# A recurrent layer's values centred as they are turned, and its output normalised without centring products

## The reference, cut to what matters

```python
state = (state * w_t[:, :, None, :] - sa[..., None] * b_t[:, :, None, :]
         + v_t[..., None] * k_t[:, :, None, :])
y_t = jnp.einsum('bhij,bhj->bhi', state, r_t)
...
mean = jnp.mean(y, axis=-1, keepdims=True)
var = jnp.mean(jnp.square(y - mean), axis=-1, keepdims=True)
y = ((y - mean) * lax.rsqrt(var + GN_EPS) * ln_w + ln_b)
bonus = jnp.sum(rh * kh * r_k, axis=-1, keepdims=True) * vh
y = (y + bonus)
return (y * jax.nn.silu(gate)) @ w_out
```

## Time and profile before

| | us |
|---|---|
| median of three runs | 1164.13 (1163.91 to 1165.45) |
| the profiled execution, its own time | 1166.54 |
| its span in the trace | 1164.4 |
| PE busy / DVE / ACT / POOL | 1130.5 / 733.9 / 608.5 / 466.5 |
| value and gate slots, then the scan's first corner | 160 to 253.8 |
| scan | 253.8 to 329.0 |
| norm stage, to the end of RWO slot 0 | 329.0 to 361.7 |

### The profile page before, as it was taken

The page is one execution under the profiler, slowest core; times in us unless marked ns, Lnnn a source line. Parts: engine busy times, 40 slices in busy tenths (PEclk is TensorE's granted clock), DMA queues, the critical chain, the costliest instruction groups (busy, mean ns, idle before and its releaser), DMA issues.

```text
span 1164.4 us, 19410 instructions
## 1 busy us (share of the span) xinstructions
PE 1130.5 (97%) x7558; PEld 888.3 (76%) x7558; DVE 733.9 (63%) x1166; ACT 608.5 (52%) x1026; POOL 466.5 (40%) x375
## 2 busy tenths in 40 slices
PE   7999999989999999999999999999999999999998
PEld 5756768878867887777777778878888888867776
DVE  6769997966675456666666484473593334567763
ACT  6867445535754466565655554462211344566563
POOL 2341024556733444333332344444454455532240
PEclk9999999999999999999999999999999999999999
DMA  8912447343183632212222123533333333322111
GB/s 279 278 55 73 88 112 219 107 136 82 45 282 99 193 105 78 85 56 73 60 68 73 55 91 92 165 90 88 98 102 91 103 97 91 91 73 67 61 55 73
DMA packets 194684, 123.02 MB, mean 106 GB/s; under 512 B 27877, under 2 KB 181030, under 8 KB 194214
## 3 DMA queue, kind: packets, MB, share of 16 engines
q1 hardware_dynamic: 191990, 119.27, 34.9%
q10 hardware_dynamic: 2608, 2.56, 0.7%
HBM read 105.03 MB, written 16.78 MB: 105 GB/s over the span
## 4 chain that ended last, share of the span: by engine, by line
PE 39%; issue 24%; POOL 12%; DVE 9%; ACT 1%; DMA 1%; POOLq 0%; ACTq 0%; SPq 0%; DVEq 0%
POOL b_w_lo L672 12%; PE banks L760 9%; PE banks L762 9%; PE banks L761 9%; DVE b_problems L2389 2%; DVE b_sum_squares L2387 2%; PE banks L1422 1%; PE banks L1020 1%; PE banks L767 1%; DVE b_a_lo L2218 1%; PE banks L1440 1%; DVE b_h_t L2214 1%; DMA b_problems<-d_a 1%; PE banks L1412 1%; PE banks L1039 1%
## 5 line engine op out<-in xcount | busy, mean ns | idle before, releaser
L672 POOL TENSOR_TENSOR b_w_lo<-b_w_raw,b_w_hi 128x512 fp32r<-128x512 f32 x296 | 401.0, 1376 | 635.6 <-ACT b_w_hi L1519 635.5
L760 PE MATMUL banks<-b_a_lo,b_w_hi 128*128 128x512 f32 x1232 | 492.5, 400 | 8.1 <-POOL b_w_lo L672 3.7
L762 PE MATMUL banks<-b_a_hi,b_w_lo 128*128 128x512 f32 x1232 | 481.6, 391 | 0.0
L761 PE MATMUL banks<-b_a_hi,b_w_hi 128*128 128x512 f32 x1232 | 480.5, 390 | 0.0
L1519 ACT ACTIVATE b_w_hi<-b_w_raw 128x1024 fp32r<-128x1024 f32 x156 | 165.1, 1058 | 259.6 <-PE banks L762 253.2
L760 PEld LDWEIGHTS banks<-b_a_lo,b_w_hi 128*128 128x128 f32 x1232 | 231.9, 188 | 70.0 <-issue 14.0
L762 PEld LDWEIGHTS banks<-b_a_hi,b_w_lo 128*128 128x128 f32 x1232 | 231.5, 188 | 50.2
L761 PEld LDWEIGHTS banks<-b_a_hi,b_w_hi 128*128 128x128 f32 x1232 | 232.1, 188 | 45.6 <-issue 0.5
L1957 ACT ACTIVATE b_exps<-banks,b_stats 128x128 f32<-128x128 f32 (+3 forms) x64 | 33.3, 525 | 67.4 <-DVE b_stats L2656 67.4
L2512 DVE SCALAR_TENSOR_TENSOR b_a_lo<-b_x_t,b_params,b_a_hi 128x512 fp32r<-128x512 f32 x32 | 34.3, 1086 | 23.5 <-ACT b_a_hi L1859 23.5
L2654 DVE TENSOR_TENSOR banks<-banks,b_consts 128x256 f32<-128x256 f32 x32 | 13.8, 433 | 45.8 <-PE banks L1269 44.7
(11 more groups left out here) (358 smaller groups left out, 1568.2 us busy)
## 6 DMA issues: line engine op xcount, KB each, us to landing
b_w_raw<-rw_w_in SPq DMA_DIRECT2D x32, 512.0 KB, 4.4
b_w_raw<-da_w_in SPq DMA_DIRECT2D x32, 512.0 KB, 4.1
b_w_raw<-w_in_a SPq DMA_DIRECT2D x32, 512.0 KB, 4.0
b_w_raw<-pe_w_gate SPq DMA_DIRECT2D x16, 512.0 KB, 4.2
d_ple<-b_ple_out SPq DMA_DIRECT2D x16, 256.0 KB, 4.2
b_w_raw<-rw_w_out SPq DMA_DIRECT2D x8, 512.0 KB, 4.2
b_ple_in<-d_ple SPq DMA_DIRECT2D x2, 2048.0 KB, 10.2
b_w_raw<-da_w_out SPq DMA_DIRECT2D x8, 512.0 KB, 3.9
```

What stands on the lines that cost most here:

```text
L672: m = pool.tensor_tensor(WLO[:, u % 2, ks], WRAW[:, u, ks], WHI[:, u % 2, ks].bitcast(F32), ALU.subtract)
L760: pe.matmul(dst, hi, a_lo[:, k_act, :], start=first, stop=False)
L761: pe.matmul(dst, hi, a_hi[:, k_act, :], start=False, stop=False)
L762: return pe.matmul(dst, lo, a_hi[:, k_act, :], start=False, stop=last)
```

## The change

The values are centred where they are turned: `turn_v` now multiplies the tile of values by the table `center` (the identity less 1/64 within each head) in place of a transposition by the identity, so what comes out is turned and free of its mean over each head. The bonus still takes the uncentred `TMP`. The eight products with `center` behind the scan are gone with their banks; ACT squares `YT` itself, and DVE multiplies `YT` by gain and gate in place. PE's embeddings are put in another order: 2 and 3 among the two sums of squares, 4 and 5 ahead of the wait for the root, 6 and 7 as before. ACT keeps embedding 2 ahead of the root. DVE does two gated bonuses ahead of the root instead of four, and the others one by one behind it.

```diff
@@ PE, turn_v
-            turn_four(BANK[6 - 2 * (j % 2)], [TMP[:, j % 2, t * P:(t + 1) * P] for t in range(TT)]).then_inc(sem("v_turn_mm"), 1)
+            for t in range(TT):
+                m = pe.matmul(BANK[6 - 2 * (j % 2)][:, t * P:(t + 1) * P], TMP[:, j % 2, t * P:(t + 1) * P], cst("center"),
+                              start=(t == 0), stop=(t == TT - 1), skip_group_check=True)
+            m.then_inc(sem("v_turn_mm"), 1)
@@ PE, behind the scan
-        for j in range(NT):
-            if j == NT - 1:
-                pe.wait_ge(sem("gn_kept"), 1)
-            if j in (2, 5):
-
-                pe.wait_ge(sem("bank_free"), RUN_RWO[1] - (1 if j == 2 else 0))
-            pe.matmul(gn_bank(j), center, YT[:, j, :], start=True, stop=True).then_inc(sem("gn_center"), 1)
-        for b in range(2):
-            gn_sums(b)
-        pe.wait_ge(sem("gn_kept"), NT)
-        for n in range(2, 5):
-            second_embedding(n)
+        second_embedding(2)
+        gn_sums(0)
+        second_embedding(3)
+        gn_sums(1)
+        pe.wait_ge(sem("bank_free"), RUN_RWO[1])
+        second_embedding(4)
+        second_embedding(5)
...
-        second_embedding(5)
         second_embedding(6)
@@ ACT
+        act.wait_ge(sem("y_even"), 2 * NC)
+        act.wait_ge(sem("y_odd"), 2 * NC)
         for j in range(NT):
-            act.wait_ge(sem("gn_center"), j + 1)
-            act.activation(GSQ[:, j, :], gn_bank(j), ACT.Square).then_inc(sem("gn_squared"), 1)
+            act.activation(GSQ[:, j, :], YT[:, j, :], ACT.Square).then_inc(sem("gn_squared"), 1)
+        keep_second(2)
         act.wait_ge(sem("gn_mm"), 2)
@@ DVE
-            stt(out=YT[:, j, :], in0=gn_bank(j), scalar=prm(LN_W, j), in1=GT[:, j, :], op0=ALU.mult, op1=ALU.mult
+            stt(out=YT[:, j, :], in0=YT[:, j, :], scalar=prm(LN_W, j), in1=GT[:, j, :], op0=ALU.mult, op1=ALU.mult
...
-        for j in range(4):
+        for j in range(2):
             gated_bonus(j)
...
-        gated_bonus(4)
+        gated_bonus(2)
...
-            if k + 5 < NT:
-                gated_bonus(k + 5)
+            if k + 3 < NT:
+                gated_bonus(k + 3)
```

More of the change, by code:

```diff
@@ L184, in sb_bank @@
     return (0, 1, 7)[i] if i < 3 else (i - 3) % 2
-def gn_tile_bank(j):
-    return (0, 1, 2, 3, 4, 5, 7, 0)[j]
 def block_rows(h, b):
@@ L357, in blocks_of @@
         return TRI0[rows_, c, :, cols] if c < 2 else TRI1[rows_, c - 2, :, cols]
-    def gn_bank(j):
-        return BANK[gn_tile_bank(j)]
     def chunk(c):
@@ L1156, in _ @@
         pe.wait_ge(sem("y_odd"), 2 * NC)
-        center = cst("center")
         def gn_sums(b):
@@ L1844, in _, with keep_second @@
         keep_y(NC - 1)
+        def keep_second(n):
+            act.wait_ge(sem("mm_done"), RUN_PLE[1][1] + n + 1)
+            if n >= 4:
+                act.wait_ge(sem(f"ple_out{n % 4}"), 48)
+            act.activation(P1OUT[:, n % 4, :], BANK[SECOND_BANKS[n]], ACT.Copy).then_inc(sem("ple_kept"), 1)
+        act.wait_ge(sem("y_even"), 2 * NC)
+        act.wait_ge(sem("y_odd"), 2 * NC)
         for j in range(NT):
-            act.wait_ge(sem("gn_center"), j + 1)
-            act.activation(GSQ[:, j, :], gn_bank(j), ACT.Square).then_inc(sem("gn_squared"), 1)
+            act.activation(GSQ[:, j, :], YT[:, j, :], ACT.Square).then_inc(sem("gn_squared"), 1)
+        keep_second(2)
         act.wait_ge(sem("gn_mm"), 2)
@@ L1888, in embed @@
                 square_tile(n0 + j, XT[:, j, :])
[L1890 to L1897, removed]
         keep_second(3)
```

## The result

The changed kernel takes 1171.39 us (median of 20 runs, 1165.74 to 1173.63) against 1165.62 (20 runs, 1163.00 to 1168.45): a ratio of 1.0044, 95% interval 1.0034 to 1.0053. It is 5.1 us slower by the ratio, where 0.2 us faster was forecast and 1166.2 was the upper end. The profiled execution took 1171.18 us, its span 1169.1 against 1164.4.

What follows compares the result with a forecast made beforehand. PE's work bounds most of the kernel, DVE's chain the value and gate slots, PE the norm stage. Value slots +2.0 and norm stage -2.2 give -0.2 on the median 1164.13: 1163.9 us, range 1161.6 to 1166.2.

Steps and rivals of the forecast that it cites:

- The value slots: Value and gate slots: dearer turns make `bonus(4)`, DVE's chain and the scan's first corner 2.0 us later, range 1.7 to 2.8.
- the better row: Price of a turn, from two places in the earlier trace: 0.45 or 0.63 us more; 0.5 was taken.
- The 1.62 us that PE stood at the corner: Scan's first corner: PE's wait for the turned blocks, subtracted from the eight turns' 3.6 us to leave 2.0.
- The rival that the turn costs its weight loads: Value slots: a turn takes 1.52 us, 1.16 more; `bonus(4)` 6.0 later, whole +3.8, 1167.9 us; chance 0.09.
- The norm stage: Behind the scan, through RWO slot 0: without the eight products of `center`, 2.2 us earlier, range 1.3 to 2.9.
- `keep_second(4)`, with its wait for the store: Norm stage on ACT: it waits for embedding 0's store, landing at 345.8, and so stays at 345.9.
- the pace of DVE: RWO slot 0: five DVE steps of 1.98 us against PE's 1.77; 2.2 us earlier, 2.9 if DVE did not pace.
- The rival that the store doesn't hold: Norm stage: embedding 0's store lands early enough, slot 0 gains 3.5 to 3.9, whole -1.7, 1162.4 us; chance 0.14.
- The step that failed: Scan's first corner: both paths reach it 2.0 us late, and the scan behind it is unchanged.
- One rival: Scan's start: PE's wait nearly vanishes, the clock stays at 2.4 GHz, 1.4 us comes back; whole -1.6, 1162.5; chance 0.16.
- The other: Norm stage: the clock falls at PE's waits, costing some 1.5 us in slot 0; whole +1.3, 1165.4 us; chance 0.11.
- the signs for a miss: Wrong if the corner moves under 1 or over 3 us, `keep_second(4)` does not wait, or PE paces slot 0.

Runs made afterwards that it cites:

- e5: Changed kernel with 192 more long-fulfilled waits on PE behind the products of the eight value slots; ratio 1.0014 to the kernel before.
- e2: Changed kernel with the old `turn_v` by transposition, so the values are not centred at all; ratio 0.9993 to the kernel before.
- e9: Changed kernel with 128 long-fulfilled waits on PE in the value slots; ratio 1.0006 to the kernel before.
- e8: Kernel before with 192 long-fulfilled waits on PE behind the products of the value slots, no other work; ratio 1.0007 to the kernel before.
- e4: Changed kernel with 192 more long-fulfilled waits on PE at the program's start, ahead of the first slot; ratio 1.0146 to the kernel before.
- e3: Kernel before with eight instructions of long-fulfilled waits behind each of the eight turns, 64 in all, no work; ratio 1.0051 to the kernel before.
- e1: Kernel before with the new `turn_v` alone, the products with `center` behind the scan still standing; ratio 1.0052 to the kernel before.
- e7: Changed kernel with half the `b_bonus_v` load behind the scan's end and embeddings 0 and 1 stored ahead of the `b_x_t` and two weight loads; ratio 1.0046.
- e6: Changed kernel, layout as it is, with half of the `b_bonus_v` load issued behind the scan's end; ratio 1.0066 to the kernel before.
- e10: Changed kernel, layout as it is, with the whole 2 MB `b_bonus_v` load issued behind the scan's end; ratio 1.0075 to the kernel before.
- e11: Changed kernel with 128 filler waits and the stores of embeddings 0 and 1 ahead of the `b_x_t` load and two weight loads; ratio 0.9999.
- e12: Changed kernel with 64 filler waits and the stores of embeddings 0 and 1 ahead of the `b_x_t` load and two weight loads; ratio 1.0029.

## Why the prediction was wrong

**The value slots: right in kind, too small.** Forecast: the corner 2.0 later, with 1.7 to 2.8. In e5, which has the layout of the kernel before and, as that, the lower clock in its first slot, the last gate product comes 2.6 later and the corner 3.3, both counted from the first product of the first slot (257.39 - 17.78 against 253.76 - 17.45):

```profile
201.28 0.69 DVE L2368 TENSOR_TENSOR b_rw_tmp<-b_rw_tmp,banks 128x512 f32<-128x512 f32 x1 [0.83 <-PE banks L846]
...
257.39 0.84 PE L1052 MATMUL banks<-b_blocks_turned,b_blocks 32*32 32x32 f32 x35 [2.28 <-DMA b_blocks_turned<-d_turned]
```

The turn costs 0.46 more and not 0.5, so the low end was the better row; eight of them are 3.7, of which 2.6 are left at the last gate product. The 1.62 us that PE stood at the corner were counted as room, but in e5 it stands 2.28, because DVE's chain is later by more than the 2.0 that `bonus(4)` was to bring. That bonus itself is only 1.5 later. Behind `bonus(5)` DVE waits for no more than 0.3 us at a time in either trace, yet its copy of the inverted blocks (`b_w_raw`) ends 2.6 later: its own operations took longer (39.2 us from the start of `bonus(5)` to the end of that copy, against 38.1). And the way from that copy through memory to the corner takes 9.1 us instead of 8.4. What stretched either was not tested. The rival that the turn costs its weight loads is refuted by 0.82 us per turn, and with it the factor of four of the Trainium skill's "TensorE: Matmul & The Clock Gate", section "Terms": here it is 2.3.

**The norm stage: right in kind, its size about as forecast.** Forecast -2.2, with -1.3 to -2.9. The changed kernel has -1.8, e2 -1.7, e5 -1.25 (30.24 us), and e9 -2.7 (28.84 against the 31.55 of e8). e4 has +0.45 (31.94): the clock was at the lower level there for 6.8 us, and in e5 for 3.4. `keep_second(4)`, with its wait for the store, and the pace of DVE came as written. The rival that the store doesn't hold is refuted.

**The step that failed** is one sentence: that both paths reach the first corner later "and the scan behind it is unchanged". The instructions that the turn adds were costed as time on PE, and not as length of PE's program; for that length the sum has no term. The kernel before holds 34 instructions between its scan's end and the end of a piece whose successor stands behind 3 MB of loads; 64 instructions more used them up. By e3 this is worth 5.9 us by itself (3.7 to 8.0): the stop, a longer way at the first corner, and the lower clock behind both. At the first corner the reason is not shown, only a pattern that overlaps: from the last gate product to the corner the six kernels with shift 64 take 4.9 to 6.7 us, those with shift 0 or 192 take 4.5 to 5.2. The three terms add within what is known of them: 2.6 - 1.8 + 5.9 = 6.7, against 5.1. If the 1.6 between are more than noise, the norm stage is the likely place: in e1 and e3, whose norm stage is that of before, the lower clock behind the stop makes it 1.6 longer (33.10 and 33.17 against 31.49), while the changed one takes 29.70 with it and 29.80 without (e2), since its wait for the store covers it (3.61 us with the lower clock, 5.34 in e2).

**The trace of before showed the risk.** It has two stops with "issue" as their end in the scan, 1.59 and 0.70 us, of which the prediction says nothing; here is the first, behind the first corner:

```profile
258.84 0.69 PE L1066 MATMUL banks<-b_blocks,b_blocks_turned 32*32 32x32 f32 x32 [1.59 <-issue]
```

A packet of the program stands at 256.4 us, 2.4 ahead of its end, as in the stops after. The place alone does not make this stop: e2 and e5, with the pieces' ends at the same instructions, do not have it.

**The clock.** One rival had the lower clock at the scan's start disappear, with the wait at the corner. The wait did not shrink, and the lower clock there lasted 6.8 us instead of 3.4; refuted for the changed kernel (of the other profiles, e7's alone has no lower clock there). The other had it fall in the norm stage, at PE's waits there. In the changed kernel it fell ahead of them, behind the stop, and by e3 the stop is enough for that. At those waits it fell in e4, e5, e6 and e10, and not in e2, e7, e9, e11 and e12, so nothing is settled on that rival in general; where it fell in e4 and e5, the norm stage took 2.1 and 0.4 us more than in e2, and 1.5 was its price. How much of the result is clock alone cannot be settled either: it differs from run to run of one kernel, in the changed one from 0.990 to 0.998 of full speed with 1173.63 to 1165.74 us, and the fall at 457 us, 1.5 us of the profiled difference, appears in e1, e3, e5 and e9 too, and in none of the other eight. Why it comes there stays open.

What was said of the signs for a miss was of use, in part by luck: the corner moved by 3.2 us, outside the 1 to 3 that the forecast allowed, but 0.5 of it stands ahead of the first slot, and the lower clock, which of the two only the kernel before has in that slot, hides some 1.5 of the rest.

## What to carry to other kernels

Count what a change adds to an engine's program, not only to its time: where an engine takes many short instructions per us, the end of a piece of program can fall into the dense part, and if large loads were issued shortly before, the engine stops for the next piece. In a profile this is idle time of PE ended by "issue" inside a run of equal products, with an instruction packet some 2.4 us ahead of its end; fillers behind products move it at no cost that could be seen (e3) and tell a change's own price from that of its layout. A comparison of two kernels that differ by some tens of instructions ahead of such a place measures the layout as well, so it is worth taking at two or three of them.

## What the runs showed of the hardware that was not expected

- PE goes on 2.3 to 2.4 us after the packet with its next piece starts: 330.9 to 333.37 (after), 330.4 to 332.70 (e3), 331.1 to 333.50 (e1), 328.0 to 330.46 (e7). The packet comes 4.3 to 6.3 us after PE has entered the piece before where 2 or 3 MB of loads stand ahead, 2.4 where 1 MB does (e10), and 1.2 in the median without them.
- All 25 stops that "issue" ends in the scans of these traces stand at a whole multiple of 256 instructions from each other.
- 64 and 192 more instructions together put the pieces' ends back: e5 has no stop in its last chunk. That its scan, 76.7 us, is as long as that of the kernel before, 76.9, where the changed kernel's is 78.7, is partly chance: e5 lacks the two stops of the kernel before and has the lower clock at the scan's start for 10.2 us instead of 3.4.
- A wait that is long fulfilled costs PE nothing behind products (0.36 us per turn with and without eight of them) and 0.11 us in the open (e4).
